# Interleaving the first slab with the rows of x, waits moved to the instruction that reads, and identity transposes around the first tiles, in a single-core decoder layer

## The chip, the core and the metric

One core of a Trainium2 chip runs the whole kernel. Its engines work from queues of their own and meet only at semaphores: PE (TensorE) multiplies and transposes, DVE (VectorE) and ACT (ScalarE) move and transform tiles, POOL (GpSimd) does a few elementwise tiles and some transfers, and SP (SyncE) issues nearly all transfers. The metric is the device time of one execution, in microseconds (us).

## The reference: what is computed

One layer for 512 tokens of width 1024, all in f32. From the reference, cut:

```python
h = rmsnorm(x, g[NORM_PRE_MIX])
(...) = split_cols(h @ w_in[l])
o_a = mla(...)      # 8 heads over a latent of width 384 + 256
o_b = dsa(...)      # 8 heads, keys chosen by top_k of an index score
o_c = nsa(...)      # 8 heads: compressed (31 keys), selected and window keys
merged = gates0 * (o_a @ w_branch0) + gates1 * (o_b @ w_branch1) + gates2 * (o_c @ w_branch2)
x = x + rmsnorm(merged @ w_out[l], g[NORM_POST_MIX])
x = x + rmsnorm(cross_attn(h, m, ...), g[NORM_POST_CROSS])
x = x + rmsnorm(jnp.square(jax.nn.relu(h @ mlp_w1[l])) @ mlp_w2[l], g[NORM_POST_MLP])
```

In `nsa` every head adds three softmax attentions, each scaled by its own gate: over 31 compressed keys, over selected blocks, over a window. Here the blocks cover all of the causal keys, so these are one causal attention with the keys `ks`, one with the keys `kw`, and a small one with 31 keys.

## The kernel before, in words

**Dense products.** Weights come as slabs of 1 MB (8 chunks of 128 rows by 256 columns) into two buffers `raw`. For each slab ACT writes a rounded copy (`weight_high`, function `high`), DVE the remainder (`weight_low`, function `low`), and a product is three matmuls per block: high with high, and each low part with the other's high (`blocks3`). A slab in the set `halved` is split in two halves, so that PE may start on the first. `low_ready` counts the halves and slabs split; SP loads slab s only when slab s-2 is split. The order of the work on each engine is written out by hand; products are numbered, and `free(g)` makes PE wait until the product two before, which had the same bank of `dense`, is taken by ACT or DVE.

**The start.** x comes in four tiles of 128 rows (512 KB each). Per tile: ACT sums the squares (L1343) and takes a root (L1322), DVE scales the rows (`x_scale`, L1801, with the gain row), PE turns them with eight transposes against `ident` (`turn_x`, L726), ACT writes `hidden_high` (`x_high`), DVE `hidden_low` (`x_low`, L1806). The first product, ("lat", 0), needs slab 0 and for its tile t of rows the hidden tile t. In the kernel before SP issues the four tiles of x and then slab 0 as one transfer; DVE splits the first half of slab 0 and POOL the second (L2319).

**Index scores.** While the latents are turned (L765) and copied by ACT to `latent_high`, PE makes the index scores in pairs (L785), ACT applies relu to them (L1395) and DVE adds them up. A pair n, n+1 with n >= 4 waits for the relu of pair n-4.

**Attention.** A pair of heads p has scores (L803, one tile per 128 queries), a softmax on DVE and ACT, and then per head: `probs` turned by PE (L813), copied by ACT to `probsT`, and multiplied with the values (L820). PE turns two parts ahead of the one it multiplies (`begin`, `finish`); the parts of a head are key tiles j = 0 to 3 with 512, 384, 256 and 128 queries. In NSA a head has nine parts: four with one kind of keys, four with the other, and the compressed one (31 rows, 512 queries, `v_cmp`) last. The values of pair p are multiplied after the first products of pair p+1, those of the last pair inside `merge(b)`, which makes a gate product ("bg") and a branch product ("bp") per 256 columns.

## Time and profile before

| what | value |
|---|---|
| median of 3 runs | 1493.57 us (1493.5 to 1493.58) |
| the profiled execution's own time | 1492.01 us |
| its span, on which all rows stand | 1490.2 us |
| PE busy | 1454.2 us, 98% of the span |
| DVE busy | 685.3 us, 46% |
| ACT busy | 568.9 us, 38% |
| POOL busy | 97.1 us, 7% |
| 16 DMA engines, mean over the span | 93 GB/s |

PE is busy for all but 36 us. So the question for an edit is which of these idle times it touches. Rows of the timeline give the start, the duration, the engine, the line, the operation, output and inputs, and in brackets how long the engine had been idle before and what released it. The columns of the page are the engine's busy share in 40 slices.

### The profile page before, as it was taken

Reading aid. Unit: us, or ns where it says so; the run is one execution under the profiler, and the core shown is the slowest. Engines: PE = TensorE matmul, PEld = TensorE weight load, DVE = VectorE, ACT = ScalarE, POOL = GpSimd, SP = SyncE. Lnnn points to the kernel's source line nnn. Section 1 sums busy time; section 2 is a strip of 40 time slices with the busy share of each in tenths; the row PEclk is TensorE's granted clock in tenths of the full one; section 3 lists DMA queues with packets and bytes.
Section 4 is the critical chain, followed back from the end, with each engine's and each line's share of the span. In section 5 each row is a group of like instructions: output and inputs, shape, how many; then the busy total and the mean of one; then the engine's idle time right before and its main releaser. Section 6 shows DMA issues by size and latency. Waiting matters only on the chain.

```text
span 1490.2 us, 17324 instructions
## 1 busy us (share of the span) xinstructions
PE 1454.2 (98%) x7180; PEld 1173.6 (79%) x7180; DVE 685.3 (46%) x1187; ACT 568.9 (38%) x920; POOL 97.1 (7%) x71
## 2 busy tenths in 40 slices
PE   6999999999999999999999999999999999999998
PEld 6967768887887788876776788897779888888886
DVE  4565657755233364454365335473354332222334
ACT  4455542224233333355345324453344332223221
POOL 1000000022120001000000101000000110012100
PEclk9999999999999999999999999999999999999999
DMA  6210222322322244540210333353121323232321
GB/s 191 76 46 31 71 86 85 113 86 71 99 68 74 66 139 144 170 128 1 71 57 29 128 113 113 97 186 113 57 85 57 113 85 113 85 111 88 104 94 57
DMA packets 118270, 137.87 MB, mean 93 GB/s; under 512 B 7043, under 2 KB 98432, under 8 KB 118192
## 3 DMA queue, kind: packets, MB, share of 16 engines
q1 hardware_dynamic: 115200, 126.17, 26.3%
q0 software_dynamic: 2704, 10.00, 1.9%
q8 instruction: 57, 0.93, 0.3%
q10 hardware_dynamic: 288, 0.59, 0.1%
q14 instruction: 21, 0.17, 0.0%
HBM read 134.61 MB, written 2.14 MB: 92 GB/s over the span
## 4 chain that ended last, share of the span: by engine, by line
PE 94%; ACT 2%; DVE 2%; issue 1%; DMA 1%; POOL 0%; SPq 0%; DVEq 0%; ACTq 0%; POOLq 0%
PE dense L669 26%; PE dense L671 25%; PE dense L670 25%; PE score L803 3%; PE turned L820 3%; PE score L820 3%; PE turned L803 2%; PE turned L813 1%; PE score L813 1%; DVE probs L1941 1%; ACT probsT L1300 1%; PE score L1198 1%; DMA raw<-in_w_in 1%; ACT weight_high L1300 0%; PE score L1184 0%
## 5 line engine op out<-in xcount | busy, mean ns | idle before, releaser
L1782 DVE TENSOR_TENSOR weight_low<-raw,weight_high 128x2048 fp32r<-128x2048 f32 (+2 forms) x96 | 201.2, 2102 | 372.0 <-ACT weight_high L1300 372.0
L669 PE MATMUL dense<-hidden_high,weight_high 128*128 128x512 f32 (+1 forms) x840 | 327.0, 389 | 4.0 <-ACT vN L1300 2.5
L671 PE MATMUL dense<-hidden_high,weight_low 128*128 128x512 f32 (+1 forms) x840 | 320.6, 382 | 0.0
L670 PE MATMUL dense<-hidden_low,weight_high 128*128 128x512 f32 (+1 forms) x840 | 320.2, 381 | 0.0
L1300 ACT ACTIVATE weight_high<-raw 128x2048 fp32r<-128x2048 f32 (+4 forms) x156 | 220.9, 1440 | 256.7 <-PE dense L671 253.8
L669 PEld LDWEIGHTS dense<-hidden_high,weight_high 128*128 128x128 f32 x840 | 158.0, 188 | 34.3 <-ACT vN L1300 2.9
L671 PEld LDWEIGHTS dense<-hidden_high,weight_low 128*128 128x128 f32 x840 | 157.9, 188 | 31.0
L670 PEld LDWEIGHTS dense<-hidden_low,weight_high 128*128 128x128 f32 x840 | 158.1, 188 | 29.7 <-issue 0.7
L1777 DVE TENSOR_TENSOR weight_low<-raw,weight_high 128x1024 fp32r<-128x1024 f32 x58 | 74.9, 1334 | 67.6 <-ACT weight_high L1300 67.6
L669 PE MATMUL dense<-weight_high,up_high 128*128 128x512 f32 x256 | 99.6, 389 | 0.0
L670 PE MATMUL dense<-weight_low,up_high 128*128 128x512 f32 x256 | 99.6, 389 | 0.0
L671 PE MATMUL dense<-weight_high,up_low 128*128 128x512 f32 x256 | 99.6, 389 | 0.0
L1405 ACT ACTIVATE probs<-probs,small 128x128 f32<-128x128 f32 (+3 forms) x128 | 70.3, 551 | 39.1 <-DVE small L1945 39.1
L669 PE MATMUL dense<-weight_high,hidden_high 128*128 128x256 f32 (+1 forms) x288 | 83.0, 288 | 2.2 <-POOL weight_low L2319 1.9
L671 PE MATMUL dense<-weight_high,hidden_low 128*128 128x256 f32 (+1 forms) x288 | 81.2, 282 | 0.0
L670 PE MATMUL dense<-weight_low,hidden_high 128*128 128x256 f32 (+1 forms) x288 | 81.2, 282 | 0.0
L669 PE MATMUL dense<-branch_out_high,weight_high 128*128 128x512 f32 x192 | 75.1, 391 | 0.0
L670 PE MATMUL dense<-branch_out_low,weight_high 128*128 128x512 f32 x192 | 74.7, 389 | 0.0
L671 PE MATMUL dense<-branch_out_high,weight_low 128*128 128x512 f32 x192 | 74.7, 389 | 0.0
L1300 ACT ACTIVATE probsT<-turned 128x512 f32<-128x512 f32 (+4 forms) x68 | 32.0, 470 | 87.7 <-PE turned L813 87.4
L803 PE MATMUL score<-kT,qT 128*128 128x128 f32 (+3 forms) x174 | 60.2, 446 | 5.2 <-DVE small L1941 2.5
L1730 ACT ACTIVATE up<-dense 128x1024 f32<-128x1024 f32 x16 | 16.5, 1029 | 112.1 <-PE dense L671 112.1
(320 smaller groups left out, 2312.9 us busy)
## 6 DMA issues: line engine op xcount, KB each, us to landing
raw<-in_w_in SPq DMA_DIRECT2D x34, 1024.0 KB, 5.2
raw<-in_mlp_w SPq DMA_DIRECT2D x32, 1024.0 KB, 5.1
raw<-in_w_branch SPq DMA_DIRECT2D x12, 1024.0 KB, 5.1
raw<-in_nsa_cmp_w SPq DMA_DIRECT2D x8, 1024.0 KB, 5.3
raw<-in_cross_wkv SPq DMA_DIRECT2D x8, 1024.0 KB, 5.4
raw<-in_w_in SPq DMA_DIRECT2D x9, 512.0 KB, 5.0
bias_strips<-bias_scratch POOLq DMA_DIRECT2D x8, 512.0 KB, 4.1
raw<-in_w_out SPq DMA_DIRECT2D x4, 1024.0 KB, 5.0
```

What stands on the lines that cost most here:

```text
L669: pe.matmul(out_ap, ah, bh, start=first, stop=False)
L670: pe.matmul(out_ap, ah, bl, start=False, stop=False)
L671: return pe.matmul(out_ap, al, bh, start=False, stop=last)
L803: mm = pe.matmul(SCORE[n % 3][:, 0:cols], q, k, start=j == 0, stop=j == len(terms) - 1)
L813: mm = pe.transpose(TURNED[m % 2][0:rows, (i - i0) * P:(i - i0 + 1) * P], probs_of(i), ident[:, :])
L820: mm = pe.matmul(ATT[att % 2][:, i0 * P:T], value, probsT[0:rows, m % 3, 0:T - i0 * P], start=first, stop=last)
L1198: mm = pe.matmul(S[m % 2][:, 0:MEM], qT[:, b, i * P:(i + 1) * P], kxT[:, 2 * n + b, :], start=b == 0, stop=b == 1)
L1300: return nc.scalar.activation(dst, src, ACT.Copy, scale=scale)
L1405: ins = nc.scalar.activation(t, t, ACT.Exp, bias=negmax[:, k:k + 1], accum_out=total[:, k:k + 1])
L1730: nc.scalar.activation(h1[:, n % 2, :, :], bank(("up", f, n))[:, :, :], ACT.Relu).then_inc(taken["A"], 1)
L1777: V.tensor_tensor(dst, src, hi.bitcast(F32), ALU.subtract).then_inc(low_ready, 1)
L1782: ins = V.tensor_tensor(dst, src, hi.bitcast(F32), ALU.subtract)
```

## The change

Seven edits, and none to the arithmetic:

1. SP issues x tile 0, the first half of slab 0 (its own semaphore `s_first`), x tile 1, the second half, then tiles 2 and 3.
2. ACT and DVE finish a tile of x before they take up the next, with the halves of slab 0 between them; DVE splits both halves, POOL none.
3. PE turns `ident` into a bank of `dense` that nothing uses yet: 16 times before x tile 0, 8 times after it, 8 times after tile 1. Tiles 2 and 3 of x are turned between the tiles of the first product.
4. ACT applies the first two relus before it copies the last latent tile; a wait of PE that the next `free` covers is left out.
5. At the three merges and in NSA PE waits for the values `vN` ahead of the value matmuls, and no longer ahead of the gate product.
6. In NSA PE waits for the compressed keys ahead of the compressed scores, and no longer ahead of all scores; DVE splits the slab ("nq", 2) behind the scores of pair 0.
7. The compressed part of a head stands fifth of nine parts and no longer last.

```diff
+            first, second = half_pieces(0, raw[0], slabs[0][0][0])
+            load_rows(0)
+            sp.dma_start(*first).then_inc(s_first, 16)
+            load_rows(1)
+            sp.dma_start(*second).then_inc(loaded[0], 16)
+            for t in range(2, NT):
+                load_rows(t)
...
+            keep_running(16)
+            turn_x(0)
+            keep_running(8)
+            turn_x(1)
+            keep_running(8)
...
-                if t == 1:
-                    turn_x(NT - 1)
+                if 1 <= t < NT - 1:
+                    turn_x(t + 1)
...
-            pe.wait_ge(taken["A"], taken_count[product_at["m4", 3]])
...
                     if n == 0:
+                        pe.wait_ge(taken["A"], taken_count[product_at[value_rows]])
                         finish()
...
-                    parts.append((16 + 6 * p + 4 + h, lambda i, h=h: probC[:, h, i, 0:NC], 0, NC, vcmp[0:NC, p // 2, :]))
+                    parts.insert(NT, (16 + 6 * p + 4 + h, lambda i, h=h: probC[:, h, i, 0:NC], 0, NC, vcmp[0:NC, p // 2, :]))
...
-                pe.wait_ge(taken["V"], taken_count[product_at["kk", r] if r else product_at["cmp"]])
+                pe.wait_ge(taken["V"], taken_count[product_at["kk", r]])
...
+                if p == 0:
+                    pe.wait_ge(taken["V"], taken_count[product_at["cmp"]])
                 for h in range(2):
                     pe.wait_ge(score_taken, n - 2)
...
+            x_norm(0)
+            act.wait_ge(s_first, 16)
+            copy(*first).then_inc(high_ready, 1)
+            x_norm(1)
+            x_high(0)
+            act.wait_ge(loaded[0], landed[0])
+            copy(*second).then_inc(high_ready, 1)
+            x_norm(2)
+            x_high(1)
+            x_norm(3)
+            x_high(2)
+            x_high(3)
             high(1)
...
             for i in range(3):
+                if i == 2:
+                    index_relu(0, 2)
                 ready(("latT", i))
...
-            nsa = 2 * causal + [(NC, T)]
+            nsa = causal + [(NC, T)] + causal
...
+            x_norm(0)
+            first_low(0)
+            x_norm(1)
             x_low(0)
+            first_low(1)
+            x_norm(2)
+            x_low(1)
+            x_norm(3)
+            x_low(2)
+            x_low(3)
             low(1)
...
-            Q.tensor_tensor(wl[0][:, c, :], raw[0][:, c, :], wh[0][:, c, :].bitcast(F32), ALU.subtract).then_inc(low_ready, 1)
```

On DVE, at the start, the rows before, from the first sum of squares to the split of the first half of slab 0:

```order
L1790 TENSOR_SCALAR small<-small 128x1 [waits x_square_sums] x2
L1798 RECIPROCAL small<-small 128x1 [waits root_done]
L1801 SCALAR_TENSOR_TENSOR x_rows<-x_rows,small,gain_row 128x1024 [waits gain_row_loaded,dve_step]
L1790 TENSOR_SCALAR small<-small 128x1 [waits x_square_sums]
L1798 RECIPROCAL small<-small 128x1 [waits root_done]
L1801 SCALAR_TENSOR_TENSOR x_rows<-x_rows,small,gain_row 128x1024 [waits dve_step]
L1790 TENSOR_SCALAR small<-small 128x1 [waits x_square_sums]
L1798 RECIPROCAL small<-small 128x1 [waits root_done]
L1801 SCALAR_TENSOR_TENSOR x_rows<-x_rows,small,gain_row 128x1024 [waits dve_step]
L1806 TENSOR_TENSOR hidden_low<-turned,hidden_high 128x8x128 [waits hidden_high_ready]
L1817 TENSOR_TENSOR weight_low_53<-raw_49,weight_high_51 128x1024 [waits slab_high_ready]
```

and the same place of the changed kernel:

```order
L1809 TENSOR_SCALAR small<-small 128x1 [waits x_square_sums]
L1817 RECIPROCAL small<-small 128x1 [waits root_done]
L1820 SCALAR_TENSOR_TENSOR x_rows<-x_rows,small,gain_row 128x1024 [waits gain_row_loaded,dve_step]
L1836 TENSOR_TENSOR weight_low_53<-raw_49,weight_high_51 128x1024 [waits slab_high_ready]
L1809 TENSOR_SCALAR small<-small 128x1 [waits x_square_sums]
L1817 RECIPROCAL small<-small 128x1 [waits root_done]
L1820 SCALAR_TENSOR_TENSOR x_rows<-x_rows,small,gain_row 128x1024 [waits dve_step]
L1825 TENSOR_TENSOR hidden_low<-turned,hidden_high 128x8x128 [waits hidden_high_ready]
L1836 TENSOR_TENSOR weight_low_53<-raw_49,weight_high_51 128x1024 [waits slab_high_ready]
```

Both halves of the slab are now split after two scaled tiles of x, where three stood ahead of the first half.

On PE, in the first head pair of NSA, the value matmuls (`probsT` times `vN` or `v_cmp`) and the transposes ahead of them, rows before, at the head's end:

```order
L820 MATMUL score<-probsT,vN 128x256 [waits probsT_ready]
L813 MATMUL turned<-ident,cmp_probs 31x128 [waits probsT_ready,probs_ready]
L813 MATMUL turned<-ident,cmp_probs 31x128 x3
L820 MATMUL score<-probsT,vN 128x128 [waits probsT_ready]
L813 MATMUL score<-ident,probs 128x128 [waits probsT_ready,probs_ready]
L813 MATMUL score<-ident,probs 128x128 x3
L820 MATMUL score<-probsT,v_cmp 128x512 [waits probsT_ready]
L813 MATMUL turned<-ident,probs 128x128 [waits probsT_ready,probs_ready]
```

and of the changed kernel, at the head's beginning:

```order
L835 MATMUL score<-probsT,vN 128x512 [waits attended_taken,probsT_ready,product_taken_by_act]
L828 MATMUL turned<-ident,probs 128x128 [waits probsT_ready,probs_ready]
L828 MATMUL turned<-ident,probs 128x128
L835 MATMUL score<-probsT,vN 128x384 [waits probsT_ready]
L828 MATMUL score<-ident,probs 128x128 [waits probsT_ready,probs_ready]
L835 MATMUL score<-probsT,vN 128x256 [waits probsT_ready]
L828 MATMUL turned<-ident,cmp_probs 31x128 [waits probsT_ready,probs_ready]
L828 MATMUL turned<-ident,cmp_probs 31x128 x3
L835 MATMUL score<-probsT,vN 128x128 [waits probsT_ready]
L828 MATMUL score<-ident,probs 128x128 [waits probsT_ready,probs_ready]
```

The compressed probabilities are now turned after the third value matmul of a head (they were turned after the seventh), and the first value matmul carries the wait for `vN`.

## Rows read from the trace of the kernel before

**Rows 1.** The page: PE's busy time, and the clock granted to it by slice

```profile
PE 1454.2 (98%) x7180; PEld 1173.6 (79%) x7180; DVE 685.3 (46%) x1187; ACT 568.9 (38%) x920; POOL 97.1 (7%) x71
PEclk9999999999999999999999999999999999999999
```

**Rows 2.** Waits of PE, whole span: us in total, times, longest

```profile
PE turned L726 <- DVE x_rows L1801: 10.2, 1, 10.2
PE score L803 <- DVE small L1941: 2.5, 3, 1.9
PE dense L669 <- ACT vN L1300: 2.5, 2, 1.4
PE dense L669 <- POOL weight_low L2319: 1.9, 1, 1.9
PE turned L820 <- ACT probsT L1300: 1.8, 4, 0.5
...
PE score L785 <- ACT index_relu L1395: 1.1, 1, 1.1
```

**Rows 3.** Timeline, the start: start us, us, engine and line

```profile
4.63 1.06 ACT L1343 ACTIVATE vN<-x_rows 128x1024 f32<-128x1024 f32 x1 [1.47 <-DMA x_rows<-in_x]
...
7.33 1.06 ACT L1343 ACTIVATE vN<-x_rows 128x1024 f32<-128x1024 f32 x1 [1.55 <-DMA x_rows<-in_x]
...
8.81 1.28 DVE L1801 SCALAR_TENSOR_TENSOR x_rows<-x_rows,small,gain_row 128x1024 f32<-128x1024 f32 x1
8.96 1.06 ACT L1343 ACTIVATE vN<-x_rows 128x1024 f32<-128x1024 f32 x1 [0.39 <-DMA x_rows<-in_x]
...
10.23 1.94 PE L726 MATMUL turned<-ident,x_rows 128*128 128x128 f32 x8 [10.23 <-DVE x_rows L1801]
...
13.50 1.06 ACT L1300 ACTIVATE weight_high<-raw 128x1024 fp32r<-128x1024 f32 x1 [0.26 <-DMA raw<-in_w_in]
...
15.87 0.39 PE L669 MATMUL dense<-weight_high,hidden_high 128*128 128x256 f32 x1 [0.28 <-DVE weight_low L1817]
...
16.56 2.86 POOL L2319 TENSOR_TENSOR weight_low<-raw,weight_high 128x1024 fp32r<-128x1024 f32 x1 [15.30 <-ACT weight_high L1300]
...
19.48 0.39 PE L669 MATMUL dense<-weight_high,hidden_high 128*128 128x256 f32 x1 [1.91 <-POOL weight_low L2319]
...
21.02 1.03 PE L726 MATMUL turned<-ident,x_rows 128*128 128x128 f32 x8
...
31.84 0.39 PE L669 MATMUL dense<-weight_high,hidden_high 128*128 128x256 f32 x1
```

**Rows 4.** DMA issues of the first 0.9 us: KB each, us to landing

```profile
ident<-in_c_ident ACTq DMA_DIRECT2D x1, 64.0 KB, 4.1
```

**Rows 5.** Timeline, the index scores on PE and their relu on ACT

```profile
87.07 0.97 PE L785 MATMUL score<-index_k,index_q 64*128 64x256 f32 x4 [1.05 <-ACT index_relu L1395]
...
87.89 0.39 ACT L1395 ACTIVATE index_relu<-turned 128x256 f32<-128x256 f32 x1 [0.59 <-DVE index_score L1910]
```

**Rows 6.** Timeline, PE, the first gate product of merges 0 and 1

```profile
204.03 0.50 PE L669 MATMUL dense<-hidden_high,weight_high 128*128 128x512 f32 x1 [1.36 <-ACT vN L1300]
...
475.27 0.50 PE L669 MATMUL dense<-hidden_high,weight_high 128*128 128x512 f32 x1 [1.11 <-ACT vN L1300]
```

**Rows 7.** Timeline, the scores of NSA's pair 0, PE and DVE

```profile
651.64 0.46 PE L803 MATMUL score<-kT,qT 128*128 128x128 f32 x2 [0.68 <-issue]
...
652.53 2.29 DVE L1782 TENSOR_TENSOR weight_low<-raw,weight_high 128x2048 fp32r<-128x2048 f32 x1 [0.99 <-ACT weight_high L1300]
...
655.09 1.13 PE L803 MATMUL score<-kT,qT 128*128 128x512 f32 x2 [1.91 <-DVE small L1941]
```

**Rows 8.** Timeline, the compressed part in NSA, DVE and PE

```profile
673.24 0.28 DVE L2121 TENSOR_REDUCE small<-cmp_probs 128x4 f32<-128x124 f32 x1
...
683.21 0.60 PE L813 MATMUL turned<-ident,cmp_probs 128*31 128x128 f32 x4
...
744.74 1.12 PE L820 MATMUL turned<-probsT,v_cmp 31*128 31x512 f32 x2 [0.45 <-ACT probsT L1300]
```

More of the change, by code:

```diff
@@ L619, in _, with load_rows @@
         def _(sp):
-            for t in range(NT):
+            def load_rows(t):
                 sp.dma_start(xN[:, t, :], out_row(a["x"])[:, t, :]).then_inc(s_x[t], 16)
@@ L727, in turn_x, with keep_running @@
                 mm.then_inc(product_ready, 1)
-            for t in range(NT - 1):
-                turn_x(t)
+            def keep_running(count):
+                for _ in range(count):
+                    pe.transpose(G[0][:, 0, 0:P], ident[:, :], ident[:, :])
+            keep_running(16)
[3 more added lines that the diff above has]
+            keep_running(8)
             def hidden_tile(t):
-                if t == 1:
-                    turn_x(NT - 1)
+                if 1 <= t < NT - 1:
+                    turn_x(t + 1)
                 pe.wait_ge(hidden_split, t + 1)
@@ L909, in _, with merge @@
                     mla_v(p)
-            pe.wait_ge(taken["A"], taken_count[product_at["m4", 3]])
-            def merge(b, last_values, after=lambda name, n: None):
+            def merge(b, last_values, value_rows, after=lambda name, n: None):
                 begin, finish = last_values
@@ L927, in merge @@
                     after("bp", n)
-            merge(0, mla_values(3))
+            merge(0, mla_values(3), ("m4", 3))
             def dsa_values(p):
@@ L986, in compress_rows @@
                         t_mode(slab_at[part_of,], two(g), both, KD, hT).then_inc(product_ready, 1)
-            merge(1, dsa_values(3), compress_rows)
+            merge(1, dsa_values(3), ("dv", 3), compress_rows)
             def turn_hidden():
@@ L1070, in _ @@
                     n += 1
-                if p % 2 == 0:
-                    pe.wait_ge(taken["A"], taken_count[product_at["vv", r]])
-            merge(2, nsa_values(3))
+            merge(2, nsa_values(3), ("vv", 1))
             def turn_memory(i):
@@ L1338, in _, with x_norm @@
             nc.scalar.activation(spare, eps, ACT.Sqrt)
-            for t in range(NT):
+            def x_norm(t):
                 act.wait_ge(s_x[t], 16)
@@ L1343, in _ @@
                 nc.scalar.activation(junk, xN[:, t, :], ACT.Square, accum_out=stat[:, t:t + 1]).then_inc(xsum_ready, 1)
-                if t:
-                    x_root(t - 1)
-            x_root(NT - 1)
-            for k, (dst, src) in enumerate(half_pieces(0, wh[0], raw[0])):
-                x_high(k)
-                act.wait_ge(loaded[0], landed[0])
-                copy(dst, src).then_inc(high_ready, 1)
-            for t in range(2, NT):
-                x_high(t)
+                x_root(t)
+            first, second = half_pieces(0, wh[0], raw[0])
+            x_norm(0)
[10 more added lines that the diff above has]
+            x_high(3)
             high(1)
@@ L1380, in _ @@
             high(slab_at["iq", 1] + 2)
-            for i in range(3):
-                ready(("latT", i))
-                for b in range(2 if i < 2 else 1):
-                    c = 2 * i + b
-                    ins = copy(latH[:, c, :], bank(("latT", i))[:, b, :], gains[:, 56 + c:57 + c])
-                ins.then_inc(lat_high, 1)
             def index_relu(first, last):
@@ L1395, in index_relu @@
                     nc.scalar.activation(relu[:, n % 2, 0:cols], INDEX[n % 4][:, 0:cols], ACT.Relu).then_inc(index_taken, 1)
-            index_relu(0, INDEX_FIRST + 4)
+            for i in range(3):
+                if i == 2:
+                    index_relu(0, 2)
+                ready(("latT", i))
+                for b in range(2 if i < 2 else 1):
+                    c = 2 * i + b
+                    ins = copy(latH[:, c, :], bank(("latT", i))[:, b, :], gains[:, 56 + c:57 + c])
+                ins.then_inc(lat_high, 1)
+            index_relu(2, INDEX_FIRST + 4)
             def exps(u, slot):
@@ L1807, in x_low, with x_norm, first_low @@
                                 hTH[:, :, c].bitcast(F32), ALU.subtract).then_inc(hidden_split, 1)
-            for t in range(NT):
+            def x_norm(t):
                 dve.wait_ge(xsum_ready, t + 1)
                 root_arg(nstat[:, t:t + 1], stat[:, t:t + 1], D).then_inc(xroot_ready, 1)
-                if t:
-                    x_scale(t - 1)
-            x_low(0)
-            dve.wait_ge(high_ready, 1)
-            c = slice(0, KD // 2)
-            V.tensor_tensor(wl[0][:, c, :], raw[0][:, c, :], wh[0][:, c, :].bitcast(F32), ALU.subtract).then_inc(low_ready, 1)
-            x_scale(NT - 1)
-            for t in range(1, NT):
-                x_low(t)
-            dve.wait_ge(low_ready, 2)
+                x_scale(t)
+            def first_low(half):
+                c = slice(half * KD // 2, (half + 1) * KD // 2)
+                dve.wait_ge(high_ready, half + 1)
+                V.tensor_tensor(wl[0][:, c, :], raw[0][:, c, :], wh[0][:, c, :].bitcast(F32), ALU.subtract).then_inc(low_ready, 1)
+            x_norm(0)
+            first_low(0)
+            x_norm(1)
+            x_low(0)
+            first_low(1)
[4 more added lines that the diff above has]
+            x_low(3)
             low(1)
@@ L2088, in _ @@
                     V.tensor_copy(vcmp[0:NC, :, :], bank("cmp")[0:NC, 1, 0:2 * P].rearrange("p (r c) -> p r c", c=P)).then_inc(taken["V"], 1)
-                    low(slab_at["vv", 0] + 2)
                 if p:
```

12 lines of the change are left out of this document (3 added, 9 removed).

## The prediction, made before the result

> **What bounds the kernel now.** I read the page first: PE is busy for 1454.2 of 1490.2 us, and the granted clock stands at its full mark in every slice [rows 1]. So the kernel is one row of matmuls, and a change that leaves their number alone can only work on the 36 us in which PE is idle. The second view is the list of PE's waits [rows 2]: 10.2 us until the first tile of x is scaled, 1.9 for POOL's half of the first slab, 2.5 for the values `vN` in two places, 2.5 for scores that DVE must take first (1.9 of it in one place), 1.8 for `probsT` in four places, 1.1 for a relu. The third is the timeline around each [rows 3 to 8]. What isn't on this list (DVE at 46%, ACT at 38%, the transfers) counts only where it would join it.
>
> **The start (edits 1 to 3).** Before, x tiles land in the places that the sums of squares show, 4.63, 7.33 and 8.96 us, and slab 0 at 13.5 [rows 3]. I keep the total and swap the order: each piece is 512 KB, so the first half of the slab takes the place of tile 1 (7.3), tile 1 that of tile 2 (9.0), the second half comes near 10.4, tile 2 near 11.8, tile 3 near 13.2 (9.0 to 13.5 is 4.5 us for three pieces and a half, some 1.4 each).
>
> Tile 0: squares end at 5.8 (1.06 and a short read behind 4.63); argument, root and reciprocal are three short instructions, together 0.6 by my estimate; the scaling starts at the latest when it did (8.81), at best near 7, when the gain row is there, and takes 1.28. PE meanwhile does its 16 transposes: `ident` is issued at 0.74 and lands after 4.1 us [rows 4], so they begin at 4.85. Eight transposes took 1.94 us at 10.23 and 1.03 us at 21.02 [rows 3]; the first rate is half of the second, so after 10.2 us of idling the engine ran at the lower of its levels (1.2 GHz, not 2.4), though the page's slice shows the full mark. Sixteen at that rate end at 8.7. Tile 0 is turned from 8.7 to 10.6.
>
> Tile 1: squares from 9.0 to 10.1, argument, root and reciprocal to 10.75, scaling to 12.05, turned from 12.1. Before, PE had worked without a break from 10.23 to 15.87, 5.6 us, and the matmuls from 15.87 on go at the full rate; counted from 4.85 the same stretch ends at 10.5. So I take the full rate for tile 1 and for the eight transposes behind it, 1.03 us each: PE reaches the first product at 14.2. `hidden_low` 0 comes at 13.3 (behind the scaling of tile 1, 1.23 us on DVE), the first half of the slab is split by 9.7, the second by 14.6; nothing of these is later than PE needs it. The first product starts at 14.2 in place of 15.87.
>
> From there to the second product it took 31.84 - 15.87 = 15.97 us [rows 3], of which 1.91 were idle until POOL's 2.86 us were over at 19.4, 2.1 with the running down of the matmul pipeline (a matmul is shown with 0.28 us, and the next starts 0.12 behind it). The gap goes, since DVE's second half is ready 1 us before PE asks. One set of eight transposes (tile 2) is new inside, 0.9. So the second product starts at 14.2 + 15.97 - 2.1 + 0.9 = 28.95, **2.9 us earlier**. The tiles behind hold: my chain for tile 2 has `hidden_low` 1 at 17.8 against PE's 18.0, for tile 3 20.95 against 21.8, and slab 1 is split by 27.1. The bounds: 1.0 if tile 1 and the identity behind it still run at the lower level (1.9 us later), 3.7 if the identity transposes cost nothing. What follows should shift with it: PE has no wait between the second product and the latents, and the splits, copies and loads there are released by PE's own products or by a split that is.
>
> The Trainium skill ("TensorE: Matmul & The Clock Gate", the part on the clock gate) says that the array starts cold at half rate, warms with sustained activity, and that the moment varies from run to run. With the first two the trace agrees, with 1.94 against 1.03 us; the last no run here shows, and by it the start might give either 2.9 or near 1.0, which is a rival below.
>
> **Index scores (edit 4).** PE waits 1.05 us for the relu of pair 0, which ACT does behind the last latent copy [rows 5]. With two relus ahead of that copy they are over when the turning of the last latent ends, and the wait goes. But the third relu waits for DVE and starts at 87.89 whatever PE does [rows 5], so the next pair may wait 0.1 to 0.2. I take **0.9**, between 0 and 1.1. The chain of relu and sum behind it idled for PE, so it can follow.
>
> **The merges (edit 5).** 1.36 and 1.11 us [rows 6], **2.5** in all, go to the value matmuls, a whole gate product later, when ACT's copy of 1 us is long done. The third merge had no such wait. What could be late next are the transposes two chunks ahead of the product's end, which want DVE's normalised probabilities; L813 is nowhere in the list of waits [rows 2], and comes 1.4 us earlier. Between 1.1 and 2.5.
>
> **Scores of NSA's pair 0 (edit 6).** PE idles 0.68 us until DVE has the compressed keys, does three tiles, and idles 1.91 because DVE first splits a slab from 652.53 (2.29 us) [rows 7]. Both go: DVE takes the first score 3.1 us earlier, right behind its two copies, and PE runs through. **2.6**. The split now stands behind the scores, so the normalising comes 2.3 later against them; the compressed probabilities were begun at 673.24 and turned at 683.21 [rows 8], so 10 us are there for it. The slab is for pair 2, far off. Between 1.9 and 2.6.
>
> **The compressed part fifth (edit 7).** Four times PE waits 0.45 for the copy of `probsT` ahead of the last value matmul of a pair [rows 2, 8], because the last part is a turn of 512 columns with just one short matmul (128 columns) to hide ACT's 0.6 us copy. At fifth place the turn of the next part hides it, and the last part is a short one as in the other branches, which don't stand in the list. **1.8**, between 0 and 1.8. The price could be that a compressed part is now turned four parts, some 3.7 us, earlier: 683.21 becomes 679.5, against 673.24 and the 1.4 us in which DVE scales it. In the last pairs, with one product less in between, I estimate the lead at 3 us.
>
> **Sum.** 2.9 + 0.9 + 2.5 + 2.6 + 1.8 = 10.7 us. The profiled execution took 1492.01, so 1481.3; its time is 1.56 below the median of the runs, 1493.57, against which I give the forecast: **1482.9**, 0.7% faster. A measurement of this kernel tells about 0.2% (3 us) from no change.
>
> **Rivals.** (a) The clock rises later than I take it: the start gives 1.0, the rest 7.8, and the time is 1484.8. For it: one stretch is all the evidence, and PE now has a break of 0.5 to 1.5 us before tile 1. Against it: 5.6 us had been enough. 0.15. (b) The gains of the start and of the index part are given back between 30 and 110 us, where DVE and ACT work in long chains and some slabs are split a few tenths before PE asks: 6.9 remain, 1486.7. Against it: those chains hang on PE's own products. 0.10. (c) A moved wait takes the place of the old: in the merges or at the compressed part DVE is late, and 2.5 + 1.8 don't come: 1487.2. For it: DVE's list of pair 0 got 2.3 us longer; against it: the 10 us above. 0.07. (d) Slower: the identity transposes don't bring the clock up and the breaks between them keep it low through the first product, from 14.2 to 29. All of PE's 14 us there would double: the start is then 11 us later in place of 2.9 earlier, the rest still gives 7.8, and the time is 1493.57 + 11.1 - 7.8 = 1496.9. It turns the sign when PE stays at the lower level for more than some 10.7 us of matmuls. Against it: the granted clock of the page is full in all slices [rows 1], and 5.6 us of transposes alone had raised the rate. 0.03.
>
> **How the numbers follow.** The forecast has 0.65. Its own range is 1481 to 1484.5, from a start that gives 3.7 down to terms that give half a microsecond less each. With (a), (b) and most of (c), 8 in 10 lie in 1480.8 to 1487. All but (d) and a part of a mixed bad case lie more than 3 us under 1493.57: faster 0.95, within 0.2% 0.03, slower 0.02.
>
> **What would show it.** PE's first dense matmul near 14.2 and the second product near 29; eight transposes of x tile 1 in about 1.0 us; POOL's split gone and no gap in the first product; no wait of the dense product on `vN`; the fourth score of NSA's pair 0 without a wait; no wait of L835 on `probsT`; PE idle for 25 to 27 us in all, with the identity transposes counted as busy 6 to 8 us less. Wrong would be: the same waits under another name, above all of a value matmul on `vN`, of a transpose on DVE's probabilities, or of the dense product on a slab's low part in the first 110 us.

## The result, and the profile after

The changed kernel takes **1480.32 us** (4 runs, 1480.05 to 1480.70), the kernel before 1493.57 (4 runs, 1493.50 to 1494.52): 13.25 us faster, ratio 0.991 with a 95% interval of 0.9893 to 0.9927. The forecast was 1482.9 with a range from 1480.8 to 1487.0. The direction was right and the waits went where the forecast said; the time lies 2.6 us under the forecast and half a microsecond under the range.

The profiled execution took 1480.70 us. Its page, the line of the span and that of the engines:

```profile
span 1478.9 us, 17387 instructions
PE 1455.6 (98%) x7212; PEld 1175.5 (79%) x7212; DVE 686.4 (46%) x1188; ACT 568.9 (38%) x920; POOL 94.3 (6%) x70
```

PE has 32 instructions more than in [rows 1] and a span 11.3 us shorter. It is idle for 23.3 us, where it was idle for 36.0. PE's waits in the profile after (us in total, times, longest), against [rows 2]:

```profile
PE dense L739 <- DMA ident<-in_c_ident: 5.5, 1, 5.5
PE score L818 <- DVE small L1967: 1.3, 4, 0.3
PE turned L733 <- DVE x_rows L1820: 1.1, 1, 1.1
PE score L733 <- DVE x_rows L1820: 1.0, 1, 1.0
PE dense L676 <- DVE hidden_low L2198: 0.9, 1, 0.9
```

The waits for POOL's half slab, for `vN`, for `probsT` and for the long 1.9 of DVE's scores are off the list. Nothing came in their place under another name, but for a small one: the score tiles of L818 wait 0.3 us four times, two of them new; with the compressed part last (an experiment below) there are again only two.

The start of the timeline after, against [rows 3]:

```profile
5.27 1.06 ACT L1354 ACTIVATE vN<-x_rows 128x1024 f32<-128x1024 f32 x1 [2.11 <-DMA x_rows<-in_x]
5.51 3.48 PE L739 MATMUL dense<-ident 128*128 128x128 f32 x16 [5.51 <-DMA ident<-in_c_ident]
...
8.78 1.28 DVE L1820 SCALAR_TENSOR_TENSOR x_rows<-x_rows,small,gain_row 128x1024 f32<-128x1024 f32 x1 [1.74 <-DMA gain_row<-in_norm_gains]
...
10.12 1.09 PE L733 MATMUL turned<-ident,x_rows 128*128 128x128 f32 x8 [1.13 <-DVE x_rows L1820]
11.05 1.04 PE L739 MATMUL dense<-ident 128*128 128x128 f32 x8
13.07 1.09 PE L733 MATMUL score<-ident,x_rows 128*128 128x128 f32 x8 [0.98 <-DVE x_rows L1820]
14.00 1.04 PE L739 MATMUL dense<-ident 128*128 128x128 f32 x8
14.79 0.36 PE L676 MATMUL dense<-weight_high,hidden_high 128*128 128x256 f32 x1
...
29.43 0.39 PE L676 MATMUL dense<-weight_high,hidden_high 128*128 128x256 f32 x1
```

Sixteen turns of the identity took 3.48 us, the eight of x tile 0 behind them 1.09: PE's rate had doubled by 10.12. The first product begins at 14.79 (before 15.87) and holds no gap; the second begins at 29.43 (before 31.84). This start is one of the later ones: in the six other profiles below that keep this start (one of them with four turns in place of the last eight), the second product begins between 28.68 and 28.95.

The places of [rows 5 to 8] in the profile after; the first is the index score that waited 1.05 us, the next two are the first gate products of merges 0 and 1, the last two the scores of NSA's pair 0 and the compressed values:

```profile
83.54 0.70 PE L800 MATMUL score<-index_k,index_q 64*128 64x256 f32 x4
...
199.43 0.40 PE L676 MATMUL dense<-hidden_high,weight_high 128*128 128x512 f32 x1
...
469.27 0.40 PE L676 MATMUL dense<-hidden_high,weight_high 128*128 128x512 f32 x1
...
645.52 1.67 PE L818 MATMUL score<-kT,qT 128*128 128x384 f32 x4
...
671.76 1.12 PE L835 MATMUL score<-probsT,v_cmp 31*128 31x512 f32 x2
```

None has a bracket, so none waits. I matched the matmuls of the two traces one by one and read by how much each stands earlier. The step in that lead, stage by stage, beside the terms of the forecast:

| stage | forecast, us | lead gained, us |
|---|---|---|
| start, to the second product | 2.9 | 2.41 |
| index scores | 0.9 | 0.65 |
| merges 0 and 1 | 2.5 | 1.67 + 1.40 = 3.07 |
| scores of NSA's pair 0 | 2.6 | 2.90 |
| compressed part, four pairs | 1.8 | 2.29 |
| sum | 10.7 | 11.32 |

The two profiled executions differ by 1492.01 - 1480.70 = 11.31 us, so the table leaves nothing over in this pair. But the medians differ by 13.25. About 2 us of the gain are not in this pair of traces, and the experiments were made for them.

### The profile page after: what moved, and what is told of

It is laid out like the page before. It is cut to its first block, busy times and chain, and to the rows that moved or that the text cites. A ratio compares the mean times of both kernels' runs of the same rounds, so it can differ in the third digit from the quotient of the medians.

```text
span 1478.9 us, 17387 instructions
## 1 busy us (share of the span) xinstructions
PE 1455.6 (98%) x7212; PEld 1175.5 (79%) x7212; DVE 686.4 (46%) x1188; ACT 568.9 (38%) x920; POOL 94.3 (6%) x70
## 4 chain that ended last, share of the span: by engine, by line
PE 95%; DVE 2%; ACT 1%; issue 1%; DMA 1%; DVEq 0%; ACTq 0%
PE dense L676 26%; PE dense L678 26%; PE dense L677 25%; PE score L818 4%; PE turned L835 3%; PE score L835 3%; PE turned L818 2%; PE turned L828 1%; PE score L828 1%; DVE probs L1967 1%; PE score L1209 1%; DMA gain_row<-in_norm_gains 1%; ACT probsT L1311 0%; PE score L1195 0%; PE turned L1195 0%
## 5 line engine op out<-in xcount | busy, mean ns | idle before, releaser
L818 PE MATMUL score<-kT,qT 128*128 128x128 f32 (+3 forms) x174 | 59.8, 445 | 3.0 <-DVE small L1967 1.3
```

Of the source, the lines that this page charges most:

```text
L818: mm = pe.matmul(SCORE[n % 3][:, 0:cols], q, k, start=j == 0, stop=j == len(terms) - 1)
```

## The experiments

The first four kernels split the change and repeat the kernel before. All kernels are timed against the kernel before on the same chip, whose medians there were 1493.68 to 1493.84.

**The kernel before, again.** No edit.

> The kernel before, run and profiled once more. The two traces show the change 11.3 us shorter, the medians 13.25, because the profiled execution of before (1492.01) lies 1.5 under the median of its runs. Theory clock: ordinary executions of before lose 1.5 us at the start, where TensorE's rate rises at a moment that varies, and the profiled one was a lucky one. Then this profile shows either 1492.0 again or 1493.5, and in the second case the second product starts near 33.4 instead of 31.84 us. Rival spread: the 1.5 us come from somewhere else, say from when the first transfers land or from many small differences, and the second product stands at 31.8 in a profile of 1493.5 too.

Measured: 1493.35 us (10 runs, 1492.19 to 1494.30), ratio 0.9997 (0.9987 to 1.0006). Its profiled execution took 1493.44, 1.43 more than that of [rows 1]. The first view is PE's timeline, the second the busy times by stretch (us, PE busy, PEld, DVE, ACT, POOL, granted clock, DMA share, GB/s), both of this kernel's start:

```profile
19.38 0.39 PE L669 MATMUL dense<-weight_high,hidden_high 128*128 128x256 f32 x1 [1.92 <-POOL weight_low L2319]
...
21.00 1.91 PE L726 MATMUL turned<-ident,x_rows 128*128 128x128 f32 x8
```

```profile
17.40:21.00 3.60, 1.68 (x14) 1.63 (x14) 1.97 (x2) 0.00 (x0) 2.38 (x2) 0.97 0.16 41
21.00:22.00 1.00, 1.00 (x6) 1.00 (x6) 0.00 (x0) 0.00 (x0) 0.00 (x0) 0.50 0.93 272
...
23.00:24.00 1.00, 1.00 (x7) 1.00 (x7) 0.00 (x1) 1.00 (x2) 0.00 (x0) 0.50 0.73 82
24.00:25.00 1.00, 1.00 (x9) 1.00 (x9) 1.00 (x1) 1.00 (x1) 0.00 (x0) 0.91 0.00 0
```

Some 1.4 us after PE came out of its wait for POOL the granted clock is 0.50 (1.2 GHz) for about three microseconds. The transposes of x tile 3 take 1.91 us, where [rows 3] has 1.03 at 21.02 in the other execution of the same program. The second product begins at 33.30 where [rows 3] has 31.84, 1.46 us later, the whole difference between the two profiled times. So the 1.92 us wait has a second price, paid in some executions: the clock goes down behind it. The execution of [rows 1] was one without it. How many of the ordinary runs have such a fall is counted below.

**Edits 1 to 3 alone.** The whole start: order of loads, the identity, the pipeline of x tiles.

```diff
-            load(0)
+            load_rows(0)
+            sp.dma_start(*first).then_inc(s_first, 16)
...
+            keep_running(16)
```

> The kernel before with edits 1 to 3 alone (order of x and slab halves, both halves split by DVE, identity transposes). By the traces the start gave 2.4 us. Theory clock: the median falls by 2.4 + 1.5 to 1.9, to 1489.3 to 1489.7, and the spread of its runs is small. Rival spread: it falls by 2.4 to 1491.2.

Measured: 1489.37 us (9 runs, 1488.96 to 1490.75), ratio 0.9975 (0.9965 to 0.9984): 4.4 us for edits that gained 2.41 in the pair of traces. The runs lie at 1489.0 to 1489.4 (five) and 1490.3 to 1490.8 (four). The profiled one took 1490.31; its timeline and stretches at the scores of NSA's pair 0, where the old wait of 1.9 us for DVE is still there:

```profile
652.01 1.13 PE L818 MATMUL score<-kT,qT 128*128 128x512 f32 x2 [1.91 <-DVE small L1969]
...
653.26 2.34 PE L818 MATMUL score<-kT,qT 128*128 128x256 f32 x4
```

```profile
650.00:652.00 2.00, 0.10 (x1) 0.00 (x0) 2.00 (x4) 0.73 (x1) 0.00 (x0) 1.00 0.00 0
652.00:654.00 2.00, 1.99 (x6) 1.18 (x7) 1.57 (x8) 0.00 (x0) 0.00 (x0) 0.78 0.52 119
654.00:656.00 2.00, 2.00 (x4) 1.11 (x4) 1.08 (x6) 1.88 (x7) 0.00 (x0) 0.50 1.14 323
656.00:658.00 2.00, 1.86 (x7) 0.97 (x6) 1.14 (x6) 0.44 (x3) 0.00 (x0) 0.87 0.34 82
```

The same thing at the other long gap: 0.50 granted from some 1.1 us behind it. The four 256-wide tiles take 2.34 us here and 1.65 in a trace in which the clock stays up. This fall is worth some 1.3 us: from the second product to its end this execution takes 1459.7 us, that of [rows 1] 1458.4, and the two groups of runs lie as far apart.

**Edits 4 to 7 alone.** The start as before.

```diff
-            pe.wait_ge(taken["A"], taken_count[product_at["m4", 3]])
...
+                    parts.insert(NT, (16 + 6 * p + 4 + h, lambda i, h=h: probC[:, h, i, 0:NC], 0, NC, vcmp[0:NC, p // 2, :]))
...
+                    index_relu(0, 2)
```

> The kernel before with edits 4 to 7 alone (relus earlier, waits moved, compressed part fifth), the start as before. By the traces these gave 8.9 us. Theory clock: the median falls by 8.9 to 1484.7. Rival spread: it falls by 10.5 to 10.8, to 1482.9.

Measured: 1485.23 us (5 runs, 1483.14 to 1486.60), ratio 0.9943 (0.9931 to 0.9956). 8.5 gained where the traces' steps 2 to 5 sum to 8.9. Beside the whole change it lacks 4.8 us, and the profiled run again shows the fall behind POOL's half slab (0.50 granted from 21 to 23 us). Its fastest run, 1483.14, lacks only 2.8, about the 2.41 of the table.

**The change without its 32 turns of the identity.**

```diff
-            keep_running(16)
             turn_x(0)
-            keep_running(8)
             turn_x(1)
-            keep_running(8)
```

> The changed kernel without its 32 identity transposes, all else kept. Theory clock: the first product begins up to 0.7 us earlier (14.1, when hidden_low is there), but at half the rate for some us, so the second product comes 1 to 3 us later than 29.4 and the time is 1481.3 to 1483.3, with more spread. Rival: the transposes do nothing but delay, and the time is 1479.6 to 1480.3.

Measured: 1481.54 us (4 runs, 1480.85 to 1481.76), ratio 0.9919 (0.9906 to 0.9933), 1.1 us behind the whole change. PE's timeline at this kernel's start:

```profile
8.92 1.94 PE L733 MATMUL turned<-ident,x_rows 128*128 128x128 f32 x8 [8.92 <-DVE x_rows L1817]
12.37 1.97 PE L733 MATMUL score<-ident,x_rows 128*128 128x128 f32 x8 [1.51 <-DVE x_rows L1817]
13.99 0.56 PE L676 MATMUL dense<-weight_high,hidden_high 128*128 128x256 f32 x1
...
18.33 0.28 PE L678 MATMUL dense<-weight_high,hidden_low 128*128 128x256 f32 x1
```

The first product begins at 13.99, 0.8 us earlier than in the profile after, though five others with all 32 added turns have it at 14.03 to 14.31. Its first matmuls take 0.41 us in place of 0.28, up to about 18 us, and the second product begins at 30.49, 1.06 us later than in the profile after and at least 1.5 later than in those five. That is what the identity buys: not an earlier product, but a full clock in it. By the medians of the runs it is worth 1.1 us.

The next kernels ask whether it is the idleness of the two long gaps that brings the clock down. On the kernel before, PE turns the identity while it would wait; nothing else moves.

**Both gaps filled; only the start's; only NSA's.**

```diff
+                            if s == 0:
+                                for _ in range(14):
+                                    pe.transpose(W[:, 0, 0:P], ident[:, :], ident[:, :])
...
+            for _ in range(4):
+                pe.transpose(OT[:, 0:P], ident[:, :], ident[:, :])
...
+                            if p == 0 and h == 0 and w == 0 and i == 3:
+                                for _ in range(13):
+                                    pe.transpose(OT[:, 0:P], ident[:, :], ident[:, :])
```

> As fill_start, and 4 and 13 identity transposes more in PE's two waits ahead of and inside the first scores of NSA's pair 0 (0.68 and 1.91 us idle). Theory clock: the fall seen in one profile at 653 us (0.9 us) goes too; all runs then lie near 1491.9 to 1492.2, with a spread under 0.6 us. Rival: as the kernel before, 1493.6, with its spread of 2.9 us.

> The kernel before with one addition: 14 identity transposes (0.13 us each at the full rate) into a bank that nothing uses, in front of PE's wait for POOL's half of the first slab. The wait still ends when it did, 19.4 us; only PE isn't idle in it. Theory clock: idle time of 1.9 us makes the clock fall for 3.4 us (seen in two of three profiles with this start, at 21.2 and 20.3 us, at 1.5 us each); without the idle time it doesn't, and the median falls by 1.5 us to about 1492.0 to 1492.2, the slowest kinds of runs (1494.2 to 1494.7) going to 1493. Rival: what the clock does there is chance and not due to the idle time: no change, 1493.6 within 0.3.

> The kernel before with identity transposes (4 and 13) in PE's two waits around the first scores of NSA's pair 0 alone; the wait for POOL's half slab at the start stays idle. Theory clock, each place by itself: the fall at 655 us goes, the one at 21 us stays: two groups near 1492.0 and 1493.5, median 0.3 to 0.6 under before. Rival, the falls replace each other: median as before within 0.3, and the profile shows the low rate at 21 us.

Measured: both 1492.56 us (11 runs, 1492.00 to 1493.60), ratio 0.9993 (0.9984 to 1.0002); the start's alone 1493.58 (11 runs, 1492.43 to 1494.96), ratio 1.0001 (0.9992 to 1.0009); NSA's alone 1493.63 (11 runs, 1492.02 to 1494.23), ratio 0.9998 (0.9990 to 1.0007). The profiled run with the start filled, at the start and at NSA's gap:

```profile
17.53 1.69 PE L699 MATMUL turned<-ident 128*128 128x128 f32 x14
19.63 0.39 PE L669 MATMUL dense<-weight_high,hidden_high 128*128 128x256 f32 x1 [0.41 <-POOL weight_low L2322]
...
21.16 1.04 PE L729 MATMUL turned<-ident,x_rows 128*128 128x128 f32 x8
...
655.19 1.71 PE L806 MATMUL score<-kT,qT 128*128 128x512 f32 x2 [1.91 <-DVE small L1944]
```

```profile
656.00:658.00 2.00, 2.00 (x7) 1.25 (x6) 1.03 (x5) 0.12 (x1) 0.00 (x0) 0.50 0.97 256
```

With the gap filled the tile behind it is turned at the full rate (1.04), and the fall comes at the gap that was left. The profiles of the other two, both filled (1493.06) and NSA's filled (1492.78), show no fall. The median of both filled is 1.1 us under the kernel before on its chip, though its interval just reaches no change. Filling one gap gives nothing that can be told in the times, against the 1.5 and 0.3 to 0.6 us that I had expected.

The granted clock says more than the times, since each run carries its mean. Over 74 runs of the kernel before, on four chips: clock 1.000, 3 runs, mean 1492.10 us; 0.999, 23 runs, mean 1492.62; 0.998, 41 runs, mean 1493.96; 0.997, 7 runs, mean 1494.72. The fastest are the ones with the highest clock, and the profiled execution of [rows 1] (1492.01, clock 0.999) lies among them. The mean also tells falls: all four profiled executions that show one read 0.998, and the twelve that show none read 0.999 or 1.000 (they miss 1.000 because every profile reads 0.50 in its last 1 to 4 us, behind PE's last matmul). So I count the runs at 0.998 or less:

| kernels | PE's waits of 1.9 us | runs at 0.998 or less |
|---|---|---|
| the kernel before | both | 48 of 74 |
| edits 4 to 7 alone; NSA's gap filled | POOL's | 4 of 5; 3 of 11 |
| edits 1 to 3 alone; the start's gap filled; edit 6 undone (below) | DVE's | 3 of 9; 7 of 11; 1 of 5 |
| both gaps filled | none left idle | 1 of 11 |
| the changed kernel and its other variants | none | 1 of 34 |

The falls go with the two gaps: 48 of 74 with both, 18 of 41 with one, 2 of 45 with none. That they also cost the time stands in the means: 1494.07 us for the 48 runs, 1492.56 for the other 26. The lone run of the last row (edit 4 undone, 1482.48 us) says, by this reading, that a fall is possible without a 1.9 us wait; it wasn't traced.

Falls aren't all of the spread. The profile with both gaps filled has none and took 1493.06, 1.05 us more than that of [rows 1]: its slab 0 was copied from 14.33 on where [rows 3] has 13.50, and its second product began at 32.70 for 31.84. Such differences of the first 15 us, up to 0.9 us, are as large as what one filled gap should have given. They may be why the times with one gap filled tell nothing; no run shows it.

The last group undoes one edit of the changed kernel each. The changed kernel stands at 1480.4 (1480.32 and 1480.48, below). In part they were timed on other chips than it, but the kernel before has the same median on all of them within 0.3 us.

**Edit 5 undone at the three merges (not in NSA): the wait for the values ahead of the gate product again.**

```diff
+                pe.wait_ge(taken["A"], taken_count[product_at[value_rows]])
                 t_mode(slab_at["bg", b, n], two(g), both, KD, hT, None if n else ahead(begin, KD)).then_inc(product_ready, 1)
                 if n == 0:
-                    pe.wait_ge(taken["A"], taken_count[product_at[value_rows]])
```

> The changed kernel with the waits for the values ahead of the gate product of the three merges again (the third never cost anything). By the idle times it should lose 2.5 us (1482.8), by the shift between the two traces 3.1 us (1483.4); if an idle time of 1.4 or 1.1 us can bring the clock down as 1.9 does, up to 3 more (1486).

Measured: 1483.33 us (5 runs, 1483.24 to 1483.64), ratio 0.993 (0.9918 to 0.9943): the edit is worth 2.9. PE's wait is back:

```profile
PE dense L676 <- ACT vN L1311: 2.5, 2, 1.4
```

It shows 2.5 us, the cost is 2.9: a gap costs more than the idle time that is shown. The matmul in flight runs down before it (a matmul is shown with 0.28 us where the next starts 0.12 behind it), and the first behind the gap isn't overlapped (0.50 us in [rows 6], 0.40 in the profile after).

**Edit 7 undone: the compressed part last again.**

```diff
-                    parts.insert(NT, (16 + 6 * p + 4 + h, lambda i, h=h: probC[:, h, i, 0:NC], 0, NC, vcmp[0:NC, p // 2, :]))
+                    parts.append((16 + 6 * p + 4 + h, lambda i, h=h: probC[:, h, i, 0:NC], 0, NC, vcmp[0:NC, p // 2, :]))
```

> The changed kernel with the compressed part last of nine again. By the four idle times it loses 1.8 us (1482.1), by the shift between the traces 2.3 us (1482.6). If the place in the row and not the last copy were without effect: 1480.3.

Measured: 1482.39 us (5 runs, 1482.30 to 1482.64), ratio 0.9924 (0.9912 to 0.9937): worth 2.0. Two rows of its waits:

```profile
PE turned L835 <- ACT probsT L1311: 1.8, 4, 0.5
...
PE score L818 <- DVE small L1967: 0.6, 2, 0.3
```

The four waits of the old order are back with 1.8, and of the four of 0.3 two are gone: so the new order brings two new waits of 0.3 us, and what it gains is net of them.

**Edit 6 undone: NSA's pair 0 begins as before.**

```diff
-                pe.wait_ge(taken["V"], taken_count[product_at["kk", r]])
+                pe.wait_ge(taken["V"], taken_count[product_at["kk", r] if r else product_at["cmp"]])
...
+                    low(slab_at["vv", 0] + 2)
```

> The changed kernel with PE's wait for the compressed keys ahead of all scores and DVE's split ahead of them again (edit 6 undone). By the idle times it loses 2.6 us (1482.9), by the shift between the traces 2.9 (1483.2); theory clock: the idle 1.9 us bring the clock down in a part of the runs, for 0.9 us or more, so that they fall in two groups near 1483.2 and 1484.3. Rival: one group.

Measured: 1484.57 us (5 runs: 1483.31, 1483.72, 1484.57, 1484.66, 1484.69), ratio 0.9939 (0.9925 to 0.9952). The profiled run is the fastest, 2.9 over the changed kernel, and its trace has the gap but no fall:

```profile
648.56 1.13 PE L818 MATMUL score<-kT,qT 128*128 128x512 f32 x2 [1.90 <-DVE small L1965]
```

Three of the five lie some 1.3 us higher. So the edit is worth 2.9 in the run whose trace shows the clock up, and about 4.2 in those. I had expected two such groups, from falls, but the clock bears it out for one run alone: the three have 1.000, 0.999 and 0.998. The first has no fall by this reading, so something else can cost as much; a start like that of the changed kernel's second profile (below) is a candidate that no trace settles. Edits 5 and 7, whose gaps are of at most 1.4 us, keep their runs within 0.4 us.

**Edit 4 undone: all relus behind the last latent copy.**

```diff
-                if i == 2:
-                    index_relu(0, 2)
...
-            index_relu(2, INDEX_FIRST + 4)
+            index_relu(0, INDEX_FIRST + 4)
```

> The changed kernel with ACT's first two relus behind the last latent copy again. By the shift between the traces 0.65 us are lost, by the idle time 1.1, by the forecast 0.9: 1481.0, 1481.4 or 1481.2 against 1480.35.

Measured: 1481.11 us (4 runs, three from 1481.02 to 1481.13 and one at 1482.48), ratio 0.9919 (0.9906 to 0.9933), 0.7 over the changed kernel; the row `PE score L800 <- ACT index_relu L1405: 1.1, 1, 1.1` is back among the waits. A wait of 1.05 us was worth 0.7: the relu chain behind it isn't shortened by the edit, and in the profile after the next four scores take 1.25 us where they take 0.70 with the edit undone.

**The changed kernel again.** No edit.

> The changed kernel once more, with more runs and on the chip of the others: 1480.3 to 1480.7 if the first four runs were typical, ratio 0.991. It has no idle time of PE over 1.1 us behind the start, so by the theory clock the runs lie in one group, within 0.7 us.

Measured: 1480.48 us (4 runs, 1480.36 to 1481.23), ratio 0.9914 (0.9901 to 0.9928). The profiled run is the slowest, 1481.23, and its start shows why:

```profile
5.25 3.67 PE L739 MATMUL dense<-ident 128*128 128x128 f32 x16 [5.25 <-DMA ident<-in_c_ident]
10.08 1.97 PE L733 MATMUL turned<-ident,x_rows 128*128 128x128 f32 x8 [1.16 <-DVE x_rows L1820]
11.85 1.80 PE L739 MATMUL dense<-ident 128*128 128x128 f32 x8
13.48 1.04 PE L733 MATMUL score<-ident,x_rows 128*128 128x128 f32 x8
...
29.77 0.39 PE L676 MATMUL dense<-weight_high,hidden_high 128*128 128x256 f32 x1
```

The same program, and here the sixteen turns of the identity didn't bring the rate up: tile 0 and the eight turns behind it still ran at half of it (1.97 and 1.80 us, for 1.09 and 1.04 in the first profile). The full rate came with tile 1, and the second product at 29.77, some 0.9 us behind the 28.68 to 28.95 of the other profiles. The moment at which the rate rises varies from one execution to the next, also in the kernel before: the eight turns of x tile 2 took 1.92 us in the profile of [rows 1] and 1.22 when it was profiled again.

**Two versions of the start.** In the first the gain row is asked for ahead of the identity, and four turns of it in place of eight stand behind x tile 1; in the second only the four turns.

```diff
             turn_x(1)
-            keep_running(8)
+            keep_running(4)
...
+            nc.scalar.dma_start(gainRow[:, :], a["norm_gains"][0, 0].partition_broadcast(P)).then_inc(s_gain, 16)
             nc.scalar.dma_start(ident[:, :], a["c_ident"]).then_inc(s_ident, 16)
-            nc.scalar.dma_start(gainRow[:, :], a["norm_gains"][0, 0].partition_broadcast(P)).then_inc(s_gain, 16)
```

> The changed kernel with the gain row issued ahead of the identity and 4 instead of 8 identity transposes behind x tile 1. In the trace of the changed kernel DVE's first scaling waits 1.74 us for the gain row (8.78), and the first product for the last identity transposes, until 14.79, 0.6 us after hidden_low. If the start is bound by these, it comes 0.3 to 0.7 us earlier: 1479.6 to 1480.0. If the chain from x tile 1 (landing at 9.3) binds it: 0 to 0.3, 1480.0 to 1480.3.

> The changed kernel with 4 instead of 8 identity transposes behind x tile 1. The first product begins at 14.3 instead of 14.8, but its second tile waits for hidden_low 1, ready at 18.2 as before: 0.3 us gained, 1480.0 against the changed kernel of the same chip; if the extra ones cost all of their 0.5 us, 0.5.

Measured: 1480.96 us (4 runs, 1480.41 to 1481.54), ratio 0.9916 (0.9902 to 0.9929), and 1480.24 (4 runs, 1480.07 to 1480.30), ratio 0.9911 (0.9896 to 0.9927). Neither can be told from the changed kernel; the first lies above the 1480.3 that I had given it at most. PE in the first of them:

```profile
7.31 3.49 PE L739 MATMUL dense<-ident 128*128 128x128 f32 x16 [7.31 <-DMA ident<-in_c_ident]
10.63 1.04 PE L733 MATMUL turned<-ident,x_rows 128*128 128x128 f32 x8
...
14.14 0.36 PE L676 MATMUL dense<-weight_high,hidden_high 128*128 128x256 f32 x1
```

Tile 0 was scaled from 7.72 on, with no wait for the gain row. The identity came 1.8 us later than in the profile after, and its sixteen turns stood in the way of tile 0, which was turned at 10.63. The first product began 0.65 us earlier than in the profile after, but not earlier than in the six other profiles with the old order of the two loads (13.88 to 14.31): there the gain row came early enough for tile 0 to be scaled between 7.41 and 8.19. The wait for it in the profile after was a matter of that execution, and the total shows nothing of the new order.

## Why the prediction came out as it did

**What bounds the kernel** held: PE's idle time fell from 36.0 to 23.3 us, and the time with it. It is 12.7 us less where the time is 11.3 less, since PE is busy for 1.4 us more, with 32 added turns. I had written 25 to 27 us of idle time.

**The start, 2.9 forecast, 2.41 in the trace.** The mechanism held step by step: identity at the lower rate (3.48 us for sixteen; 3.9 assumed), tile 1 at the full rate, no gap in the product. The first product came at 14.79 for 14.2, the second at 29.43 for 28.95. What was late is the chain on DVE: the scaling of tile 0 waited until 8.78 for the gain row (I had left that between 7 and 8.8), the split of the half slab came behind it, and tile 1 was scaled at 11.73. The other profiles of this start have tile 1 at 10.97 to 11.26 and the second product at 28.68 to 28.95, so the term was right for them, measured against the 31.84 of [rows 3]. The transfers, too, landed some 0.6 us later than I took them (`ident` at 5.5 for 4.85, the squares of tile 0 at 5.27 for 4.63), but this varies: the squares begin at 4.67 to 5.27 in the profiles with this order of loads (the one with the gain row first aside) and at 4.63 to 5.24 in those with the old.

**Index scores, 0.9 forecast,** 0.65 by the trace and 0.7 by undoing: the give-back of 0.1 to 0.2 was 0.4.

**Merges, 2.5 forecast,** 3.07 and 2.9. **NSA's pair 0, 2.6 forecast,** 2.90, and 2.9 or 4.2 by undoing. **Compressed part, 1.8 forecast,** 2.29 and 2.0. In these three I summed the idle time as shown. In the start I had added 0.2 us to POOL's gap for the running down of the pipeline, and didn't apply my own correction to the other gaps; by the traces the three terms were short by 0.6, 0.3 and 0.5 us, 1.4 in all, of which the start and the index took back 0.7. Nothing was late in their place, as rival (c) had it, but for the two new waits of 0.3.

**The step that failed is the last of the sum:** "its time is 1.56 below the median of the runs, 1493.57, against which I give the forecast". I took these 1.56 us for a constant that would stand over the changed kernel too. They were no constant but for the most part a cost of the gaps themselves: falls of the clock behind the two waits of 1.9 us, which the profiled execution happened not to have and 48 of 74 ordinary runs have, at 1.5 us more on average. The change removes both gaps and so this cost. Of the 16 profiled executions of this study four show a fall while PE has work, two behind POOL's half slab (in four that have this gap) and two behind DVE's scores (in five that have that one), and none anywhere else; the changed kernel's two profiles have none, none of its eight runs reads 0.998 or less, and they lie within 1.2 us, for 3.6 in the 74 of before. The miss of 2.6 us is: 0.6 from the terms, 1.56 from the offset, 0.38 because the changed kernel's profiled run lay above its own median, where the earlier one lay below. The 0.38 is of the size of that profile's late start, some 0.5 us.

The range took in the bounds of the terms, but no bound for the offset. Left free between 0 and 1.56 us, it moves the low end from 1480.8 to 1479.2, and the range holds the time. The 1481 that I gave as the low end of the forecast's own range didn't follow either: all five terms at their upper bounds sum to 11.7 us, which is 1481.9.

**The rivals.** (a), the clock rising later: real, but smaller than I priced it. In the first profile the eight turns at 10.12 took 1.09; in the second the rate rose only at tile 1, which cost 0.9 us against the other profiles, and no profile with the added turns shows tile 1 at the low rate, for which (a) took 1.9. (b), gains given back between 30 and 110 us: only the 0.4 of the index part. (c): no. (d), slower: the opposite, the clock was full through the first product; without the identity it was low to about 18 us, not to 29.

**What is open.** 13.25 is 11.31 by the stages, 1.56 by the offset before and 0.38 by the one after. That a fall costs such an offset is shown for a single execution (1.46 us lost in the profile of the kernel before, again). That the ordinary runs have falls, and lose them with the gaps, is shown by the counts of their granted clock; that it brings the whole 1.56 at the medians is not, since both gaps filled brought 1.1 us with an interval that reaches no change, and the first 15 us of an execution add up to 0.9 us of their own. Why a 1.9 us wait brings a fall in some executions and not in others, and why the times with one gap filled show no gain, was not settled.

## What to carry to other kernels

A profiled execution that lies under the median of the runs is a finding and not an offset: look for what the ordinary runs have that it hasn't, before its difference is carried over to a changed kernel. One profile of a start stands for one execution: the same start put the second product anywhere from 28.68 to 29.77 us here, with no fall in it. A gap of TensorE may cost a second time in what the clock does behind it, so the longest gaps are worth more than their idle time, here 1.9 us idle and up to 1.5 more behind it. And to each gap that goes, add the running down of the pipeline, 0.1 to 0.3 us here.

## What the runs showed of the hardware

- In some executions a wait of 1.9 us on PE was followed, 0.3 to 1.4 us behind its end, by a granted clock of 0.50 for about 3 us (21 to 24 us, and 653 to 657 in another kernel). In others, of the same program, it was not. Behind shorter gaps (1.7 us and less, once the kernel had left the low level of its start) no profile here showed one, though one run without a longer gap has the mean clock of a fall (0.998, edit 4 undone).
- At the start the granted clock of the stretches reads 1.00 although the first turns take 1.94 us for eight, at any later place 1.04 (the kernel without the identity has eight in 1.97 at 12.37 and 0.41 us a matmul to 18 us). The lower level of the start is read from durations alone: the trace has no entry for the clock before the rate rises, which is at 8.66 us in the profile after, at 13.4 in the changed kernel's second and at 18.2 in the one without the identity, and the view shows 1.00 where there is none.
- After how long the rate rises varies: of the nine profiles that turn the identity sixteen times first, eight have tile 0 wholly or for the most part at the full rate, one only tile 1.
- The page's row of the granted clock shows 9 in every slice even with a fall of 3 us inside: a slice is 37 us long. The mean over the run (0.998 with one fall, 0.999 or 1.000 without) told them.
- Which DMA is asked for first on ACT's queue decides by 1.8 us when a 64 KB transfer lands at the start: the identity came at 5.51 (4.94 to 5.31 in the other profiles), and behind the gain row, which is 512 KB, at 7.31.
